# Splitting the next weights and half of the next factor before the last piece is moved out, and pooling between the pieces of xbc, in a two-block Trainium2 kernel

## The reference, cut to what matters

```python
# block 1
u = modulate(rmsnorm(h), ...);  proj = u @ w_in
y_conv = conv_module(p_conv) ; o = gla(q, k, v, logg)
y_gla = (o * silu(r)) @ w_gla_o
merged = gt[0] * y_conv + gt[1] * y_gla
h = h + ga1 * (merged @ w_out)
h = h + ga2 * hierarchical_moe(u2, ...)          # 32 experts, top 2
# block 2
q, k, v, pool_in, z, xbc, dt, gate_pre = split(rmsnorm(x) @ w_in_2)
y_a = dilated_attention(q, k, v) @ w_a
for window in (2, 4, 8, 16):                      # one group of 256 channels each
    d = (c - shifted) / count - pool_in           # c: running sum over time
y_b = (d @ w_grp * scale) @ w_b
y_c = ssd_mixer(z, xbc, dt, ...) @ w_c
merged = gates[0] * y_a + gates[1] * y_b + gates[2] * y_c
x = x + merged @ w_o
x = x + (silu(conv(u3 @ w_up_a)) * conv(u3 @ w_up_v)) @ w_down    # u3 = rmsnorm(x)
return rmsnorm(x)
```

## Time and profile before

| | |
|---|---|
| median of 3 runs | 1574.64 us (1572.33 to 1578.69) |
| profiled execution: time / span | 1575.1 us / 1573.3 us |
| granted TensorE clock, mean | 0.885 |
| PE busy / PEld busy | 1261.5 us (80%) / 996.3 us (63%) |
| DVE / ACT busy | 681.6 us (43%) / 454.1 us (29%) |
| DMA | 374.02 MB, 238 GB/s over the span |
| expert loads | 240 + 144 of 512 KB |

### The profile page before, as it was taken

How to read it: one execution, slowest core, us unless ns; L and a number is a source line. 1 busy time by engine, 2 the same in 40 slices (tenths; PEclk the granted TensorE clock), 3 DMA queues, 4 the chain that set the end, 5 groups by cost and what they waited for, 6 DMA issues and landing times. The chain is left out here.

```text
span 1573.3 us, 21069 instructions
## 1 busy us (share of the span) xinstructions
PE 1261.5 (80%) x9022; PEld 996.3 (63%) x9022; DVE 681.6 (43%) x1146; ACT 454.1 (29%) x645; POOL 1.9 (0%) x15
## 2 busy tenths in 40 slices
PE   6889987797766566675665689999798888899897
PEld 3679976686413112131121389899698788899897
DVE  3547983553300000000000355355547675678854
ACT  2433342433000000000000343334345443445442
POOL 0000000000000000000000000000000000000000
PEclk7999989798888787777788889899899999999999
DMA  9786620886999999999999756434343334355450
GB/s 355 246 274 200 212 81 8 276 278 253 397 388 398 391 394 398 387 398 394 390 398 389 260 184 185 134 116 127 107 152 115 122 108 138 113 178 187 145 205 28
DMA packets 226426, 374.02 MB, mean 238 GB/s; under 512 B 8838, under 2 KB 121880, under 8 KB 226200
## 3 DMA queue, kind: packets, MB, share of 16 engines
q1 hardware_dynamic: 226160, 369.05, 66.3%
q0 software_dynamic: 144, 3.54, 0.7%
q10 hardware_dynamic: 24, 0.03, 0.0%
HBM read 371.51 MB, written 4.62 MB: 239 GB/s over the span
## 5 line engine op out<-in xcount | busy, mean ns | idle before, releaser
L547 PE MATMUL bank<-fine 128*128 128x256 f32 x4656 | 592.1, 290 | 62.1 <-DVE fine L1135 49.1
L547 PEld LDWEIGHTS bank<-fine 128*128 128x128 f32 x4656 | 582.2, 198 | 72.1 <-issue 61.7
L1135 DVE TENSOR_TENSOR fine<-arena,fine 128x1024 fp32r<-128x1024 f32 (+1 forms) x257 | 298.1, 1190 | 192.1 <-ACT fine L1855 182.9
L1855 ACT ACTIVATE fine<-arena 128x1024 fp32r<-128x1024 f32 (+2 forms) x279 | 266.1, 984 | 204.7 <-PE bank L547 123.9
L1855 ACT ACTIVATE arena<-bank 128x256 f32<-128x256 f32 (+2 forms) x157 | 71.5, 479 | 611.8 <-PE bank L825 195.2
L814 PE MATMUL bank<-arena 128*32 128x512 f32 x640 | 106.5, 804 | 75.1 <-DMA arena<-in_w 75.1
L1135 DVE TENSOR_TENSOR arena<-arena,bank 128x512 f32<-128x512 f32 x8 | 5.5, 688 | 302.1 <-PE bank L814 302.0
L1855 ACT ACTIVATE arena<-arena 128x512 f32<-128x512 f32 (+6 forms) x99 | 66.8, 705 | 184.9 <-DVE arena L1135 92.5
L814 PEld LDWEIGHTS bank<-arena 128*32 128x32 f32 x640 | 20.7, 128 | 154.0 <-DMA arena<-in_w 103.4
L1143 DVE SCALAR_TENSOR_TENSOR arena<-arena 128x256 f32<-128x256 f32 (+2 forms) x261 | 105.4, 472 | 0.3
L814 PE MATMUL bank<-above,arena 128*32 128x512 f32 x384 | 61.1, 772 | 40.1 <-DMA above<-in_w 40.1
(11 more groups left out here) (158 smaller groups left out, 823.0 us busy)
## 6 DMA issues: line engine op xcount, KB each, us to landing
arena<-in_w SPq DMA_DIRECT2D x240, 512.0 KB, 11.7
above<-in_w SPq DMA_DIRECT2D x144, 512.0 KB, 11.5
arena<-in_w_in SPq DMA_DIRECT2D x62, 1024.0 KB, 5.5
arena<-in_w_ada SPq DMA_DIRECT2D x24, 1024.0 KB, 7.8
arena<-in_ffn_w_up SPq DMA_DIRECT2D x22, 1024.0 KB, 5.1
arena<-in_ffn_w_down SPq DMA_DIRECT2D x11, 1024.0 KB, 4.9
arena<-in_w_ada_f SPq DMA_DIRECT2D x8, 1024.0 KB, 9.2
arena<-in_w_gla_o SPq DMA_DIRECT2D x4, 1024.0 KB, 8.5
```

The costliest lines, as they stand in the source:

```text
L547: ins = e.matmul(o, w[:, k, j * P:j * P + P], x[:, kt, :], start=start, stop=stop, skip_group_check=True)
L1135: return e.tensor_tensor(o, a, b, f)
L1855: return e.activation(o, i, f, bias=bias, scale=scale)
```

## The change

On VectorE and ScalarE, at merged1, py, ys, merged2 and w_down: the first piece of the next matrix is split (`advance`) before the last piece is moved out; then the first half of the next factor; then `flush(2)` moves the last piece out, and the second half of the factor follows. xbc's first piece is split right behind the attention loop. Pooling becomes a generator, whose steps stand between the splits of xbc's pieces. TensorE waits for u2 and u3 tile by tile. The diff, cut:

```diff
+        TILE_BY_TILE = ("u1", "u2", "u3")
@@ tensor_program, make
-                if p.i == 0 and FIRST[FACTOR[p.name]] == p.name:
+                first = p.i == 0 and FIRST[FACTOR[p.name]] == p.name
+                if first and FACTOR[p.name] not in TILE_BY_TILE:
                     e.wait_ge(*x_lo_v[FACTOR[p.name], half])
...
+                        if first and j == 0 and FACTOR[p.name] in TILE_BY_TILE:
+                            e.wait_ge(*x_lo_v[FACTOR[p.name], "tile", kt])
@@ vector_program, norm_split
-                    ins.then_inc(*x_lo_v.up((name, k // 4) if k % 4 == 3 else None))
+                    ins.then_inc(*x_lo_v.up((name, "tile", k)))
@@ vector_program, merged1
             advance("gla_o", 3)
-            flush()
             advance("w_out", 1)
-            for g in range(2):
-                x_low("merged1", gates, g)
+            x_low("merged1", gates, 0)
+            flush(2)
+            x_low("merged1", gates, 1)
@@ vector_program, behind the attention loop
+            advance("xbc", 1)
             e.wait_ge(*exps[11])
...
-            flush()
-            advance("xbc", 1)
...
+            def pooling():
...
+                tt(p1[:, :, 8:264], p0[:, :, 8:264], p0[:, :, 7:263], ALU.add).then_inc(*pooled.up("p1"))
+                yield
+                e.wait_ge(*pooled["p1"])
+                tt(p2[:, 2:8, 8:264], p1[:, 2:8, 8:264], p1[:, 2:8, 6:262], ALU.add).then_inc(*pooled.up("p2"))
+                yield
+                for g in range(4):
+                    if g == 2:
...
+                        yield
...
+                    yield
+
+            steps = pooling()
+            for n in (1, 1, 2, 2, 1):
+                advance("xbc", 1)
+                for _ in range(n):
+                    next(steps, None)
@@ vector_program, ys and merged2
             advance("w_b", 2)
             for g in range(2):
+                if g:
+                    advance("w_c", 1)
                 rr = Lbs[g][:, 0:256]
...
-            flush()
-            advance("w_c", 1)
-            for g in range(2):
-                x_low("ys", ys, g)
+            x_low("ys", ys, 0)
+            flush(2)
+            x_low("ys", ys, 1)
             advance("w_c", 3)
-            flush()
             advance("w_o", 1)
-            for g in range(2):
-                x_low("merged2", merged, g)
+            x_low("merged2", merged, 0)
+            flush(2)
+            x_low("merged2", merged, 1)
@@ vector_program, w_down
             advance("up", 21)
-            flush()
+            down_low(0)
+            flush(1)
+            down_low(1)
+            down_x_low(0)
+            flush()
@@ scalar_program, w_down
             advance("up", 21)
-            flush()
+            down_high(0)
+            flush(1)
+            down_high(1)
+            down_x_high(0)
+            flush()
```

More of the change, by code:

```diff
@@ L1681, in vector_program @@
                 e.tensor_copy(yaF[:, :, tc * P:tc * P + P], shaped(bank_of(yaF_out, tc)[:, 0:384], 3, P)).then_inc(*yaF_out.up(tc))
[L1682 to L1700, removed]
@@ L1702, in vector_program @@
+            steps = pooling()
[3 more added lines that the diff above has]
+                    next(steps, None)
+            for _ in steps:
+                pass
             flush()
@@ L1826, in vector_program, with down_low, down_x_low @@
             advance("up", 21)
-            flush()
-            for i in range(11):
+            def down_low(n):
+                hi, lo = w_parts[1][(2 * NPIECES + n) % NU]
+                e.wait_ge(*down_hi["w", n])
+                tt(lo, w_down[n // 2][:, n % 2, :], hi.bitcast(F32), ALU.subtract).then_inc(*down_v.up(("w", n)))
+            def down_x_low(i):
                 at = 2 * (i % 4)
@@ L1832, in vector_program @@
                    ALU.subtract).then_inc(*down_v.up(("x", i)))
[L1833 to L1837, removed]
+            down_low(0)
[3 more added lines that the diff above has]
+            flush()
+            for i in range(11):
+                if i:
+                    down_x_low(i)
+                    down_low(2 * i)
+                    down_low(2 * i + 1)
             for m in range(8):
@@ L2245, in scalar_program, with down_high, down_x_high @@
             advance("up", 21)
-            flush()
-            for i in range(11):
+            def down_high(n):
+                if n % 2 == 0:
+                    e.wait_ge(*ring_in[load_at["down", n // 2] % NS]["down", n // 2])
+                if n < NU:
+                    e.wait_ge(*products_of[NPIECES - (NU - n + 1) // 2, n % 2])
+                else:
+                    e.wait_ge(*down_done[n - NU])
+                act(w_parts[1][(2 * NPIECES + n) % NU][0], w_down[n // 2][:, n % 2, :], ACT.Copy).then_inc(*down_hi.up(("w", n)))
+            def down_x_high(i):
                 at = 2 * (i % 4)
                 if i < 4:
-                    e.wait_ge(*products_of[NPIECES - 1, 1])
+                    e.wait_ge(*products_of[NPIECES - 1, i // 2])
                 else:
@@ L2254, in scalar_program @@
                 act(x_hi[1][:, at:at + 2, :], hidF[:, 2 * i:2 * i + 2, :], ACT.Copy).then_inc(*down_hi.up(("x", i)))
[L2255 to L2260, removed]
+            down_high(0)
[3 more added lines that the diff above has]
+            flush()
+            for i in range(11):
+                if i:
+                    down_x_high(i)
+                    down_high(2 * i)
+                    down_high(2 * i + 1)
             norm_rows(5, lambda pair: last_v["h", 2 * pair + 1])
```

18 lines of the change are left out of this document (17 added, 1 removed).

## The result

| | before | after |
|---|---|---|
| median of the runs | 1576.66 us (1572.33 to 1579.44) | 1539.32 us (1538.83 to 1540.71) |
| ratio, 95% interval | | 0.9767 [0.9741, 0.9793] |
| profiled execution's span | 1573.3 us | 1537.4 us |
| granted clock, mean | 0.885 | 0.888 |

The kernel is 2.3% faster: 37.3 us on the medians, 35.9 us between the two profiled spans. The forecast was 1536.5 us, 2.8 us too low. 2.0 us of that is the kernel before, whose median was 1574.64 us when the forecast was made and is 1576.66 us beside this result; the gain itself, 38.1 us forecast, came within 0.8 us. That small difference hides larger ones: most waits shrank as worked out, but the lower clock came back at a place that the change doesn't touch.

A forecast was written before the change was run, and what follows sets the result against it. Transfers were taken to bound the expert stage and TensorE's standing still the rest. Seven terms summed to 37.6 us, giving 1537.0 us on the median, or 1536.5 with half of ys's open 1.5 us; range 1530 to 1546.

The forecast's parts named there:

- xbc: At xbc's start: early first split and spread pooling remove waits of 2.57 and 9.22 us, plus clock loss; 13.5 us gained.
- py: Join behind gate2: three of four splits on VectorE move under gate2's products; 3.4 us gained.
- ys: Join ahead of w_c: TensorE starts at 1286.35 in place of 1289.45, 3.1 us gained, a 1.9 us wait remaining.
- The open clock term: At ys: whether the remaining 1.9 us wait still drops the clock; between 0 and 1.5 us further gain, taken as 0.
- merged2: Join ahead of w_o: wait falls from 5.01 to 0.9 us, and 2.0 us of clock returns; 6.1 us gained.
- w_down: Join behind up: 5.6 us of wait and 1.4 of clock go, 6.9 us gained, with a margin of 0.2 us.
- merged1: Join ahead of w_out: the 2.18 us wait goes, 2.1 us gained, and the expert stage moves with it.
- the slower rival: Expert stage: the stream, starting 2.1 us earlier, meets other traffic and runs slower; 1592 at 355 GB/s; chance 0.02.
- u2 and u3: TensorE starts on the first x tile, not the fourth, at both places: 1.2 to 1.3 us each, 2.5 us gained.
- The case in which each wait breaks the pulling ahead of weight loads: At u2 and u3: tile waits stop early weight loads; each place loses 0.3 us instead of gaining 1.2.
- The prediction's own sign of being wrong: A wait in xbc behind a pooling step, the clock at 0.50 behind a short wait, or expert loads at another rate.
- The clock keeps its losses: Rival: short waits drop the clock, losing 2.0 us at merged2 and 1.4 at w_down again; about 1540.5; chance 0.12.

The follow-up runs named there:

- pool_short: Kernel after, with pooling left out except for four differences of two tiles each; 1540.32 us.
- xbc_only: Kernel before with only the edits behind the attention loop: early split of xbc's first piece and pooling spread between pieces; 1560.34 us, ratio 0.9881.
- joins_only: Kernel before with only the five joins changed (merged1, py, ys, merged2, w_down); 1553.95 us, ratio 0.9845.
- pool_block: Kernel after, with pooling again in one block ahead of xbc's second piece, the early first split kept; 1546.12 us.
- xbc_late: Kernel after, pooling spread, but xbc's first piece split where it was before, behind dt and the last move out; 1539.04 us.
- no_tiles: Kernel after without the tile by tile waits: u1, u2 and u3 wait for a half again; 1541.77 us.
- best: Kernel after with the ys order changed and gate1's third piece split on VectorE ahead of the convolution's last block; 1531.83 us, ratio 0.9715.
- ys_order: Kernel after with another order at ys: both norms first, weight and x splits behind; ScalarE's gate of branch 2 moved earlier; 1537.04 us.
- best_filled: The kernel best plus 22 filling transposes in TensorE's wait ahead of the SSD state products; 1530.29 us, ratio 0.9703.
- after_again: The kernel after itself, unchanged, run again beside three other variants on one chip; 1539.91 us.
- no_wdown: Kernel after with the last join as before: both engines move out all of up before they split w_down; 1548.27 us.

## Why the prediction was right, and where a term was off

**Right in its sum, with some luck.** 37.6 us were said from one profiled execution, 35.9 us came between the profiled spans. The seven steps gave 38.2; 3.0 us lost at a place that the sum didn't have, 0.6 us more ahead of xbc and of w_c, and 1.4 us of luck in the first 330 us make the difference. Each step by the table above:

- *xbc*, 13.5 said, 14.14 measured. Both waits went and their clock with them; the walk through the five pieces held, and pool_short shows that the cover is whole. The new waits that I put into both queues (dt's chain, the attention output) stayed hidden under gate0's last 72 matmuls: VectorE's part of it ended at 1100.2, TensorE asked at 1101.28, a margin of 1 us as worked out.
- *py*, 3.4 said, 2.69 measured. The splits moved as said, but the last two groups of SSD outputs ran at the lower clock behind waits of 3.83 and 1.54 us: from the first of them to w_b's start 5.47 us, 4.75 before. The term left out the clock, because it looked at the join's wait alone.
- *ys*, 3.1 said, 3.10 measured, and the 1.9 us wait that was to remain is 1.90. The open clock term, between 0 and 1.5 us, came out at 0, the value in the sum (the forecast of 1536.5 had taken about half of it).
- *merged2*, 6.1 said, 5.92 measured: 1.08 us of wait remains (0.9 said), and the clock stays up, 168 matmuls in 20.39 us.
- *w_down*, 6.9 said, 5.61 + 1.51 = 7.12 measured, and 7.4 by its removal. The margin of 0.2 us held: VectorE's last split ended at 1456.21, TensorE starts at 1456.46.
- *merged1*, 2.1 said, 2.29 measured. The expert stage moved with it and kept its length (0.05 us of difference): the slower rival's stream still runs at 393 GB/s.
- *u2 and u3*, 2.5 said, 1.72 + 1.19 = 2.91 measured, 0.5 of it the clock in the norm ahead of u2, which no edit touches. The waits fell by 1.19 us each. The case in which each wait breaks the pulling ahead of weight loads (the Trainium skill, "TensorE: Matmul & The Clock Gate", Part 2) would have been a loss of 0.3 us at each place; no run shows it.

**What failed** is the step that hung each clock loss on its own wait, and so counted clock gains only where a wait goes. The prediction had seen that a 2.57 us wait cost nothing and a 2.34 us one did, and took this as an open size at ys. It is open at every wait behind the first edit: the SSD opening's 2.78 us wait was in neither the parts nor the rivals, since nothing there was edited, and it cost 3.0 us after costing nothing before. The prediction's own sign of being wrong, the clock at 0.50 behind a short wait, showed there and at w_c. The rival "The clock keeps its losses" named the sign and 4 us, but put them at merged2 and w_down, where the trace shows none of them. Of the Trainium skill, "TensorE: Matmul & The Clock Gate", section "A second HAM failure mode: psum-queue depth-cycling", it is borne out that small idle times make the clock swing: waits of 1.90 to 2.78 us cost 1.5 to 3.0 us each in some places, and nothing in others. It does not say which do; the 1.08 us wait ahead of w_o's second half never did.

**What stays open.** What exactly in the place decides: behind the same 2.78 us wait, with the same code right ahead of it, the four matmuls take 1.99 us before, 1.98 in xbc_only, joins_only and pool_block, 2.49 in xbc_late, 2.70 in no_tiles and 3.78 after (and 3.66 in best, where gate1's wait ahead of it is gone). The outcome repeats where TensorE's work since u2's norm is the same and changes where it isn't; no run here says how to foretell it. Also open is why kernels that are the same until there differ by up to 5.0 us at the last products of the experts (881.90 in ys_order, 886.87 in best_filled). The traces say where it comes from: 4.8 us of it are there at w_in's first product (40.34 and 45.13 us), ahead of which TensorE waits for loads of the modulation weights for 2.6 us in the one and 4.4 us in the other. Why these loads land differently, no run shows.

## What to carry to other kernels

Splitting the next operands ahead of moving out the last result works when the buffers allow it: walk each engine's queue in time, and the lengths of waits come out within a few tenths of a microsecond. Judge each part by the difference of starts of the same instruction, not by the median alone, which also holds what differs ahead of the edit: with waits of 2 to 3 us left behind it, the clock elsewhere can take a part's gain or add to it. Where such a wait can't be removed and TensorE has a free bank, try a filler of useless matmuls just shorter than the wait; it kept the clock at both places where it stood here.

## What the runs showed of the hardware

- Behind waits of equal length, in the same code, TensorE's granted clock stays at 1.00 or falls to 0.50. It repeats from run to run and from chip to chip where TensorE's work ahead is the same (3.78 us in after, after_again, pool_short, no_wdown and ys_order; 27.64 to 27.66 for w_c's 216 in the first four), and also when the whole program stands up to 4.4 us later (1184.96 in ys_order, 1189.33 in no_wdown). Where the work ahead of it is 2 to 3 us longer since u2's first product, it comes out another way (xbc_late: 5.98 us for the 48 matmuls in place of 7.47).
- 22 small transposes of 128x128, 2.56 us, into a bank that the next product overwrites, kept the clock at 1.00 through a wait behind which it was 0.50 without them.
- A matmul that waits for its tile in the middle of a stream costs nothing that a trace shows: the waits ahead of u2 and u3 fell by the whole 1.19 us, and 432 matmuls with such waits took 53.71 us, without them 53.44 (before) and 54.68 (no_tiles).
